# The v projection of a hybrid SSD/gMLP step: four weight tiles at once over five PSUM banks, with conv tiles between them

## What is computed

```python
h = rms_norm(x, norm_w) * (1 + scale) + shift
proj = h @ w_in          # 1024 -> 2048 (xbc) + 1024 (z_m) + 32 (dt) + 3*1024 (u, v, z_g) + 2*1024 (gates)
# SSD branch: centred 5-tap depthwise conv + silu on xbc, chunked scan in both directions, gated RMSNorm
# gMLP branch:
u = gelu(u_raw); v = layer_norm(gelu(v_raw))
s = einsum('gts,bnsgc->bntgc', w_sp, v) + b_sp
y_g = u * s * silu(z_g)
merged = sigmoid(gl_m) * (y_m @ w_out_m) + sigmoid(gl_g) * (y_g @ w_out_g)
x = x + gate * (merged @ w_out)
```

## Time and profile before

| | |
|---|---|
| runs shown | 1434.37, 1430.94, 1433.82 us; median 1433.82 |
| profiled execution | 1430.54 us, span 1428.8 us |
| TensorE (PE) busy | 1412.0 us, 99% of the span |
| weight loads (PEld) busy | 1373.1 us, 96% |
| POOL (GpSimd) busy | 1025.9 us, 72% |
| DVE (VectorE) busy | 991.0 us, 69% |
| ACT (ScalarE) busy | 461.9 us, 32% |
| granted TensorE clock, mean | 0.998 |

### The profile page before, as it was taken

One profiled execution on the slowest core, in us unless ns is written; L12 is line 12 of the kernel. 1 busy time (PEld: TensorE's weight loads), 2 busy tenths in 40 slices (PEclk: granted clock), 3 DMA queues, 4 the chain that ended last, 5 costly groups with the idle time before them and its releaser, 6 DMA issues.

```text
span 1428.8 us, 26989 instructions
## 1 busy us (share of the span) xinstructions
PE 1412.0 (99%) x10111; PEld 1373.1 (96%) x10111; DVE 991.0 (69%) x1470; ACT 461.9 (32%) x1054; POOL 1025.9 (72%) x1421
## 2 busy tenths in 40 slices
PE   8999999999999999999999999999999999999997
PEld 5999998999999999999999999989999999999997
DVE  5865676664777678989979677667566876868234
ACT  4332123313766333001243322231256662310122
POOL 1688875696555589998859897658765556979772
PEclk9999999999999999999999999999999999999999
DMA  9112755123566565444332245721346665453222
GB/s 361 61 64 74 188 164 167 58 61 116 157 193 181 157 257 195 142 163 143 115 133 75 79 140 151 212 74 59 92 136 187 173 191 194 147 184 118 74 74 89
DMA packets 166575, 200.03 MB, mean 140 GB/s; under 512 B 55232, under 2 KB 129088, under 8 KB 165056
## 3 DMA queue, kind: packets, MB, share of 16 engines
q1 hardware_dynamic: 89328, 148.84, 32.6%
q10 hardware_dynamic: 77136, 49.63, 11.9%
HBM read 175.03 MB, written 23.40 MB: 139 GB/s over the span
## 4 chain that ended last, share of the span: by engine, by line
PE 96%; DVE 2%; DMA 1%; ACT 0%; SPq 0%; issue 0%; POOL 0%; ACTq 0%; DVEq 0%; POOLq 0%
PE acc L624 78%; PE acc L591 6%; PE X L856 2%; PE X L821 2%; PE X L591 2%; PE X L841 1%; PE X L887 1%; PE X L867 1%; PE acc L742 0%; DMA xr<-in_xT 0%; DVE ssq L1437 0%; DVE h_pre L1489 0%; DVE xr L1964 0%; PE X L828 0%; PE X L801 0%
## 5 line engine op out<-in xcount | busy, mean ns | idle before, releaser
L536 POOL CAST w_hi<-w_st 128x256 fp32r<-128x256 f32 x704 | 417.2, 606 | 380.8 <-issue 168.2
L540 POOL TENSOR_TENSOR w_lo<-w_st,w_hi 128x256 fp32r<-128x256 f32 x704 | 646.6, 928 | 0.0
L624 PE MATMUL acc<-h_hi,w_hi 128*128 128x320 f32 x1744 | 405.3, 314 | 0.8 <-ACT h_hi L1048 0.8
L624 PE MATMUL acc<-h_lo,w_hi 128*128 128x320 f32 x1744 | 397.8, 309 | 1.2 <-DVE h_lo L1483 1.2
L624 PE MATMUL acc<-h_hi,w_lo 128*128 128x320 f32 x1744 | 397.2, 309 | 0.0
L624 PEld LDWEIGHTS acc<-h_hi,w_hi 128*128 128x128 f32 x1744 | 289.0, 188 | 10.7 <-issue 7.7
L624 PEld LDWEIGHTS acc<-h_lo,w_hi 128*128 128x128 f32 x1744 | 291.2, 188 | 1.9 <-DVE h_lo L1483 1.7
L624 PEld LDWEIGHTS acc<-h_hi,w_lo 128*128 128x128 f32 x1744 | 291.6, 188 | 0.0
L1644 DVE SCALAR_TENSOR_TENSOR cv<-raw,convw_sb,cv 128x642 f32<-128x642 f32 x128 | 133.8, 1045 | 4.5
L1396 DVE SCALAR_TENSOR_TENSOR ada_acc<-ada_st,sc,ada_acc 128x512 f32<-128x512 f32 x112 | 106.4, 989 | 1.8
L1146 ACT ACTIVATE cvt<-cv 128x642 f32<-128x642 f32 x32 | 23.8, 743 | 179.5 <-DVE cv L1644 179.5
(11 more groups left out here) (254 smaller groups left out, 2397.0 us busy)
## 6 DMA issues: line engine op xcount, KB each, us to landing
w_st<-in_wts SPq DMA_DIRECT2D x176, 512.0 KB, 3.6
cum_bc<-cum_dram ACTq DMA_DIRECT2D x80, 256.0 KB, 4.8
ada_st<-in_wada SPq DMA_DIRECT2D x33, 512.0 KB, 4.4
ex_bc<-ex_dram ACTq DMA_DIRECT2D x64, 128.0 KB, 3.1
ada_pre<-in_wada SPq DMA_DIRECT2D x15, 512.0 KB, 9.7
xs<-xs_dram SPq DMA_DIRECT2D x64, 80.0 KB, 2.5
mga_dram<-c_buf SPq DMA_DIRECT2D x16, 320.0 KB, 5.7
xf<-xf_dram SPq DMA_DIRECT2D x4, 1280.0 KB, 7.0
```

The costliest lines, as they stand in the source:

```text
L536: nc.gpsimd.tensor_copy(quarter(w_hi, slot, q), quarter(w_st, slot, q)).then_inc(s_pool, 1)
L540: nc.gpsimd.tensor_tensor(quarter(w_lo, slot, q), quarter(w_st, slot, q), f(quarter(w_hi, slot, q)), ALU.subtract).then_inc(w_split, 1)
L624: last = mm(a[:, hf, 0:n1], w[:, s, cols], x[:, k, hf * HALF:hf * HALF + n1], start=(k == 0 and n == 0), stop=(k == KC - 1 and n == 2))
```

## The change

Eight v tiles now form two groups of four (`VT = 4`): 3, 4, 6, 8 and 13, 15, 17, 19, with conv tiles at 5, 7 and 14, 16, 18. Four weight tiles are loaded quarter by quarter, a matmul moves 512 columns (128 of each), and a group makes 240/2 = 120 matmuls: 30 per tile instead of 60. The five token blocks take five whole banks: `X[0]`, `X[1]`, `X[3]` (first group) or `X[2]` (second), and both banks of one accumulator, which the group holds from its first to its last tile; the conv tiles between all use the other one. The gelu of a group is one instruction of 1024 columns and three of 512.

With that move: a v tile waits for three split quarters before its first matmul (one before) and for the fourth halfway; the decay sums stand behind tile 9 in both layers, their DVE work at the conv of tile 9 and ACT's exponentials at tile 11; the state bursts run from (20, 2) to (30, 2), five single ones and sixteen at three a tile, and the first waits for the gelu of the second group, since it writes `X[2]`; `pbb` goes from (26, 8) to (27, 8), the scan on DVE one tile later; the last x channels are turned at tiles 26 and 27; SP issues the `wsp`/`pbb` loads that ACT issued; `xs` lies in another place.

```diff
-V_AT = (3, 4, 9, 10, 15, 16, 22, 23)
+V_AT = (3, 4, 6, 8, 13, 15, 17, 19)
+VT = 4
+VKS = KC // VT
...
-A_AT = [(18 + a, 2) for a in range(7)] + [(25 + a // 3, 2 + 3 * (a % 3)) for a in range(14)]
+A_AT = [(20 + a, 2) for a in range(5)] + [(25 + a // 3, 2 + 3 * (a % 3)) for a in range(16)]
+CUMS_AT = V_AT[VT - 1] + 1
...
-V_BANK = (1, 1, 3, 1)
-PBB_AT = (26, 8)
+V_BANK = (3, 2)
+PBB_AT = (27, 8)
...
+            outs = ((2, X[0][:, :]), (3, X[1][:, :]), (4, X[V_BANK[j]][:, :]), (0, a[:, 0, :]), (1, a[:, 1, :]))
...
+            for i in range(VKS):
+                k = VKS * part + i
+                pe.wait_ge(w_split, WQ * t + 3 + i)
...
+                for c, out in outs:
+                    if k == 0 and c == 4:
...
+                            pe.wait_ge(cum_ready, L + 1)
+                    if k == 0 and c == 0:
+                        acc_ready(t)
                     for n, (w, x) in enumerate(((w_hi, h_hi), (w_lo, h_hi), (w_hi, h_lo))):
+                        last = mm(out.rearrange("p (t n) -> p t n", t=VT), x[:, k, P * c:P * (c + 1)],
+                                  w[:, s, :].rearrange("p (t k n) -> p k t n", t=VT, n=P)[:, i, :, :],
...
         def dt_cums2(L):
             pe.wait_ge(tm_ready, L + 1)
+            pe.wait_ge(v_made, 2 * L + 1)
...
                 if a == 0:
-                    pe.wait_ge(cum_ready, L + 1)
+                    pe.wait_ge(v_made, 2 * (L + 1))
...
-                if p == (2, 6)[L]:
+                if p == CUMS_AT:
                     dt_cums2(L)
...
-                    j, half = divmod(V_AT.index(p), 2)
-                    if half == 1:
+                    j, part = divmod(V_AT.index(p), VT)
+                    if part == VT - 1:
...
+                        for c, bank in ((2, 0), (3, 1), (4, V_BANK[j])):
+                            last = A(v_tok[:, g, c, :], X[bank][:, :].rearrange("p (g n) -> p g n", n=P),
+                                     ACT.Gelu_apprx_tanh)
+                        last.then_inc(v_made, 1)
```

More of the change, by code:

```diff
@@ L66, in accumulator_uses @@
             t = L * NT + p
-            if p in V_AT[1::2]:
-                uses[t] = uses[t - 1]
+            if p in V_AT:
+                if V_AT.index(p) % VT == 0:
+                    first = t
+                    take(t)
+                    at = 1 - at
+                uses[t] = uses[first]
                 continue
             take(t)
-            at = 1 - at
+            if not any(V_AT[i] < p < V_AT[i + VT - 1] for i in range(0, len(V_AT), VT)):
+                at = 1 - at
             if p == 0:
@@ L148, in order_act @@
     out += [(8 * p + k + 0.5, what, n) for (p, k), what, n in STANDS if p > T_UZ and what in ("a", "b")]
-    out += [(8 * 27 + 4, "root", 0)] + [(8 * p + k + 5, "yghi", j) for j, (p, k) in enumerate(SP_AT)]
+    out += [(8 * 25 + 4, "store", 7), (8 * 27 + 4, "root", 0)] + [(8 * p + k + 5, "yghi", j) for j, (p, k) in enumerate(SP_AT)]
     return [(what, n) for at, what, n in sorted(out)]
@@ L156, in order_dve @@
     out += [(8 * (T_G + 2 * j + 2) + 1, "og", j) for j in range(8)]
-    out += [(8 * p + k, "a", n) for n, (p, k) in enumerate(A_AT) if 9 <= n < NU]
+    out += [(8 * p + k, "a", n) for n, (p, k) in enumerate(A_AT) if 7 <= n < NU]
     out += [(8 * 25 + 3 + 3 * c, "bn", c) for c in range(NCH)] + [(8 * 26 + 7.5, "var", 0), (8 * 27 + 5, "rv", 0),
-                                                                             (8 * 27 + 1.5, "pbb", 0)]
-    out += [(8 * 27 + 6 + 3 * c, "ln", c) for c in range(NCH)] + [(8 * (30 + i) + 1.5, "scan", i) for i in range(6)]
+                                                                             (8 * 28 + 1.5, "pbb", 0)]
+    out += [(8 * 26 + 1, "turn", 6), (8 * 27 + 1, "turn", 7)]
+    out += [(8 * 27 + 6 + 3 * c, "ln", c) for c in range(NCH)] + [(8 * (31 + i) + 1.5, "scan", i) for i in range(6)]
     for j, (p, k) in enumerate(SP_AT):
@@ L263, in build @@
     dtw = place("dtw", [P, KC, 32], r_c + TOK * 4)
-    xs = [place(f"xs{i}", [P, NCH, 4, 32], r_c + i * TOK * 4) for i in range(2)]
+    xs = [place(f"xs{i}", [P, NCH, 4, 32], r_uz + (6 + i) * TOK * 4) for i in range(2)]
     xw = place("xw", [P, 2, 2, HPG, HD], r_c + 2 * TOK * 4)
@@ L420, in weight @@
             if p in V_AT:
[L421 to L423 removed]
+                n, part = VKS * P, V_AT.index(p) % VT
+                dst = dst.rearrange("p (t n) -> p t n", t=VT)
+                src = wts[at - part:at - part + VT, :, n * part:n * (part + 1)].rearrange("t p n -> p t n")
             sp.dma_start(dst, src).then_inc(w_landed[slot], 16)
@@ L476, in _ @@
                 x_gather(L, XG_AT[p])
+            if p == XG_LAST + 1:
+                for half in xf_stored:
+                    sp.wait_ge(half, 32 * KC // 2 * (L + 1))
+                sp.dma_start(wsp_sb[:, :, :], wsp[L, :, :, :]).then_inc(wsp_in, 16)
+                sp.dma_start(pbb[:, :, :].rearrange("p g n -> p (g n)"), bsp[L:L + 1, :].partition_broadcast(P))\
+                    .then_inc(wsp_in, 16)
             j = (p - T_G - 5) // 2
@@ L568, in acc_ready, with v_tile @@
                 pe.wait_ge(acc_free[at], n)
[L570 to L575, removed]
+        def v_tile(t, part, ready=None, hooks=()):
+            j, L = V_AT.index(t % NT) // VT, t // NT
+            a, s = acc_of(t), t % 2
+            outs = ((2, X[0][:, :]), (3, X[1][:, :]), (4, X[V_BANK[j]][:, :]), (0, a[:, 0, :]), (1, a[:, 1, :]))
+            if part == 0:
                 if j > 0:
-                    pe.wait_ge(v_made, KC // 2 * (t // NT) + j)
+                    pe.wait_ge(v_made, 2 * L + j)
                 if ready is not None:
                     pe.wait_ge(hpre_ready, 8 * (ready[2] + 1))
[L580 to L583, removed]
+            step = 0
+            for i in range(VKS):
+                k = VKS * part + i
+                pe.wait_ge(w_split, WQ * t + 3 + i)
                 if ready is not None:
@@ L932, in _ @@
                 rows, more = ((p_hi, p_lo), 2) if raw_rows else (h, 0)
+                ready = (hhi_ready, h_ready, L) if L > 0 and RAWT <= p < RAWT + 3 else None
                 if p in V_AT:
-                    v_tile(T0 + p, V_AT.index(p) % 2, hooks=hooks,
-                           ready=(hhi_ready, h_ready, L) if L > 0 and p < RAWT + 2 else None)
-                else:
-                    tile(T0 + p, *rows, hooks=hooks, more=more)
-                if p == (2, 6)[L]:
+                    v_tile(T0 + p, V_AT.index(p) % VT, hooks=hooks, ready=ready)
+                else:
+                    tile(T0 + p, *rows, ready=ready, hooks=hooks, more=more)
+                if p == CUMS_AT:
                     dt_cums2(L)
@@ L1186, in _ @@
                 free(t, last)
-                if i == (4, 5)[L]:
+                if i == 7:
                     act.wait_ge(cum_ready, L + 1)
@@ L1206, in _ @@
                     dt_log()
+                if p in XS_AT:
+                    x_store(XS_AT[p])
                 copies(p + 1)
                 conv_tanh(i)
[L1209 to L1213, removed]
             def load_cum(b):
@@ L1235, in _ @@
                     a_copies(n)
+                elif what == "store":
+                    x_store(n)
                 elif what == "root":
@@ L1801, in _ @@
                     scan(n)
+                elif what == "turn":
+                    x_turn(n)
                 elif what == "uz":
```

51 lines of the change are left out of this document (20 added, 31 removed).

## The result

| | before | changed |
|---|---|---|
| median of 10 runs, us | 1432.1 (1430.6 to 1434.4) | 1435.2 (1434.0 to 1436.5) |
| profiled execution, us | 1430.5 | 1435.6 |
| its span, us | 1428.8 | 1433.8 |

The ratio of the runs is 1.0024, 95% interval 1.0015 to 1.0032: 3.1 to 3.4 us slower, where +0.6 was forecast. That is under 0.3% and inside the range, but more than the measurement's own uncertainty. A second measurement of the same kernel gave 1.0021 (1.0011 to 1.0030). The two profiled executions lie 5.0 us apart, because the one of before was among the shortest of its kernel.

A forecast was written before the change was run, and what follows sets the result against it. PE was taken to bound the kernel (96% of the span), time being a sum of matmul spacings. Terms -6.4 + 5.3 + 1.2 + 1.0 - 0.5 = +0.6 us on a mean of 1432.4 gave 1433.0 us, range 1426.5 to 1440.0.

The forecast's parts named there:

- v tiles: Four v groups with 512-column matmuls: each v tile goes from 7.20 to 6.80 us, -6.4 us in all.
- stop at (20, 2): First state burst in tile 20: PE waits for ACT's last gelu, 2.65 us per layer, +5.3 us.
- tile 7, second layer: PE waits for ACT's copies of tile 5, delayed by a table load of 1.28 us; +1.2 us.
- POOL's third quarter: Tile 13 waits for the third split weight quarter, 0 to 0.9 us per layer, taken as 0.5; +1.0 us.
- wait for `xf_dram`: ACT's wait for this store, in the chain at tile 25's burst, moves to SP; about -0.5 us, once.
- bursts in tiles 18 to 31: Extra DVE turns and burst units in tiles 25 to 28 were called covered, at no cost.
- the spacing: 512-column float32r matmuls of the v tiles: 0.2267 us each, extrapolated from a straight line through 256, 320 and 384 columns.
- ACT's old wait: ACT's wait for the `xf_dram` store before u/z work, at tile 25's burst, moves to SP; about -0.5 us.
- the rivals on the spacing: v matmuls at 0.215 us, no fixed part (1429.1 us, chance 0.17), or 0.240, nothing saved (1437.4 us, chance 0.05).
- the lower bound of 2.3 us for the stop: At (20, 2), +2.3 instead of +5.3 us if the three gelus overlap as the first two and the load hides.
- my list of what would prove me wrong: Spacing 0.215 or 0.24; (20, 2) wait under 1.5 us; POOL releasing several v tiles per layer; DVE burst waits, tiles 24 to 29.

The follow-up runs named there:

- e_copy: Changed kernel with, in the second layer only, tile 5's raw copies ahead of the third convolution's tanh on ACT; 1433.7 us, ratio 0.9994 to the kernel before.
- e_burst8: Changed kernel with the first state burst of both layers behind chunk 8 of tile 20, not chunk 2; 1428.3 us, ratio 0.9945 to the kernel before.
- e_burst4: Changed kernel with the first state burst behind chunk 4 of tile 20, not chunk 2; 1429.6 us, ratio 0.9960 to the kernel before.
- e_burst3: Changed kernel with the first state burst behind chunk 3 of tile 20, not chunk 2; 1432.1 us, ratio 0.9982 to the kernel before.
- e_bank: Changed kernel whose first burst waits only for the gelu of the bank it writes, which ACT computes first; 1429.1 us, ratio 0.9954 to the kernel before.
- e_fill: Changed kernel with nine unread 512-column products ahead of the first burst's wait in both layers; 1433.5 us, ratio 0.9996 to the kernel before.
- after: The changed kernel itself in its first measurement and profile; median 1435.2 us, ratio 1.0024 to the kernel before.
- after_again: The changed kernel unchanged, measured and profiled once more beside others on the same chip; 1435.6 us, ratio 1.0021 to the kernel before.
- e_six: Changed kernel with first burst at chunk 8, tile 5's copies ahead of the tanh, six single bursts then fifteen by three; 1425.3 us, ratio 0.9952 to before.
- b_stop: Kernel before with one added PE wait behind chunk 2 of tile 22, for the tanh of tile 20's convolution; 1437.1 us, ratio 1.0038 to the kernel before.

## Why the prediction was wrong

Terms in the span of the profiled execution, both layers together:

| term | forecast | measured |
|---|---|---|
| v tiles | -6.4 | -6.1 (16 tiles of 6.80 to 6.83, POOL's share left out) |
| stop at (20, 2) | +5.3 | +5.3 (2.6 and 2.7) |
| lower clock behind it | none | +2.9 (two falls; with one of them spared, as in `e_copy`, 1.4 less) |
| tile 7, second layer | +1.2 | +1.3 |
| POOL's third quarter | +1.0 | +0.3 (first layer alone) |
| wait for `xf_dram` | -0.5 | -0.5 |
| bursts in tiles 18 to 31 | 0 | +1.6 |
| sum | +0.6 | +4.8; the traces differ by 5.0 |

**Four terms held:** the spacing, the stop, tile 7, and ACT's old wait. So did the rejection of the rivals on the spacing: 0.2267, neither 0.215 nor 0.240. The sign of the sum was right too, but I had called +0.6 no change, and it came out at over five times that. In the length of the stop two small misses offset in part: ACT's tanh ended 0.5 us behind tile 19, not 0.4, and the four gelus took 2.5 us, not 2.7.

The rule of the Trainium skill on the gap (TensorE: Matmul & The Clock Gate, N/2.4 ns plus 2.5) gives 0.2158 at 512 columns; for float32r the row of the v tiles says 0.2267, so the line through 256, 320 and 384 columns holds a third beyond its last point. Two readings in the prediction are off and change nothing in the sum: by that rule the saving would have been 11.6 us, not 11.8, and the lower bound of 2.3 us for the stop takes in only the overlap of the gelus; with the table load hidden as well it is about 1 us.

**The step that failed** is the pricing of the stop: "So PE stands still for 2.65 us per layer: **+5.3 us**". It took a wait to cost its length, and put what comes behind it at nothing. The two waits were 2.6 and 2.7 us long and cost 4.1 and 4.3, because the products behind them ran at half the clock. Five runs bear this out from different sides: the loss goes with the stop (`e_burst8`), the slow products go when the stop is shortened (`e_burst4`, `e_burst3`, `e_bank`), and they go when it is filled with work while the burst stays (`e_fill`). A sixth, `e_copy`, has the price alone: the same stop without a fall, and a tile 1.4 us shorter. The Trainium skill says why in general (the same page, The HAM clock gate): the gate sets the array's clock by how busy PE has been of late, on a rhythm of its own that isn't tied to the kernel's start. The traces agree as far as they go: the granted clock is 1.00 ahead of the stop and 0.5 from about its end, and the moment isn't fixed to the stop (0.3 us ahead of its end in `after`, 0.1 us behind it in `after_again`). I had not drawn that consequence for this wait.

**The second step** is "DVE gets two turns (0.84 each) and two burst units more in tiles 25 to 28, where PE's tiles last 9.5 to 10.5 us; covered." It was not: 16 bursts instead of 14 at three a tile, now in tiles 25 to 30, met DVE in tile 26 and a store on ACT in tile 29, 0.7 and 0.9 us per layer. That was also on my list of what would prove me wrong. `e_six` took out 1.8 us in these tiles. POOL made up for part of it: its third quarter was late by 0.3 us once, not 0.5 twice.

**What stays open:** whether a given stop lowers the clock. In the profiled executions it fell behind five of eight stops of 2.6 us or more (both of `after` and `after_again`, one of two in `e_copy`, none of two in `b_stop`), and behind none of eight in tile 20 that were 1.8 us or shorter. Why the two of `b_stop` were spared, by their moment, by the 256-column products around them or by chance, no run separates. The medians differ by 3.1 to 3.8 us while the profiled executions differ by 5.0. In part this may be falls of the clock in other executions of the kernel before (mean clock 0.995 to 0.998); but at the same mean clock of 0.997 its times still lie up to 6 us apart, and no trace shows why.

## What to carry to other kernels

A wait of a tensor-bound kernel's PE for ACT costs its length and may cost half as much again by the clock, so price it from both rows: the hole itself, and the spacing of the products behind it. When a change lets an accumulator group span more banks, ask who next writes each bank: here six chunks' delay of one transpose was worth 8.5 us, more than the 6.1 that the wider matmuls saved. And where small bursts stand close, read what the slower engines do between two neighbouring ones; here it was two DMA issues on ACT.

## What I had not expected of the hardware

- The granted clock fell behind a stop of 2.6 us in mid-kernel, after some 177 us at 1.00: products 0.265 us apart instead of 0.147 for about 3 us, 1.4 us lost. Nine products that nobody reads, put into each stop, made the two tiles 20 2.3 us shorter.
- Where the clock falls differs between executions of one kernel: tile 20 of the first layer took 11.22, 11.36 and 9.81 us with the same stop (the third is `e_copy`, which is the changed kernel up to there).
